# The pooling layer of a four-part decoder step: trailing sums on one engine, one channel group after the other

## The reference

```
h = rmsnorm(x, norm_mix)                        # x: rows x 2048
ext = concat(15 earlier rows (zeros or the stored ones), h)
for g, w in enumerate((2, 4, 8, 16)):           # four groups of 512 channels = 4 tiles
    mean = (sum of the last w rows of ext) / min(w, pos + 1)
    d[g] = mean - h                             # for the group's channels
    y[g] = d[g] @ w_pool[g]                     # 512 x 512
x = x + y * scale
new pool state = last 15 rows of ext
```

## Time and profile before

| | us |
|---|---|
| median of 3 runs | 2839.45 (2839.45 to 2842.92) |
| the profiled execution | 2834.88 |
| its span | 2833.1 |
| PE busy in it | 2645.6 (93%) |
| DVE busy | 1637.4 (58%) |
| ACT busy | 1298.8 (46%) |
| POOL busy | 511.2 (18%) |

### The profile page before, as it was taken

One profiled execution on the slowest core, in us unless ns is written; L12 is line 12 of the kernel. 1 busy time (PEld: TensorE's weight loads), 2 busy tenths in 40 slices (PEclk: granted clock), 3 DMA queues, 4 the chain that ended last, 5 costly groups with the idle time before them and its releaser, 6 DMA issues.

```text
span 2833.1 us, 68041 instructions
## 1 busy us (share of the span) xinstructions
PE 2645.6 (93%) x25416; PEld 2545.9 (90%) x25416; DVE 1637.4 (58%) x2721; ACT 1298.8 (46%) x1995; POOL 511.2 (18%) x822
## 2 busy tenths in 40 slices
PE   3899999999999699999788888889999999999997
PEld 2899999999999699999677777779999999999997
DVE  7666546664565686533554554434766456654664
ACT  1566434443344355433454545533666344443542
POOL 4222102220022300000021222222222012200222
PEclk7999999999999899999899999979999999999998
DMA  3554444444444544454010001034545454555444
GB/s 114 171 165 156 162 157 156 155 159 159 150 162 136 179 139 152 156 160 150 8 33 30 26 26 37 22 140 141 179 159 171 163 164 161 164 165 166 159 146 142
DMA packets 113711, 378.13 MB, mean 133 GB/s; under 512 B 12080, under 2 KB 22960, under 8 KB 113328
## 3 DMA queue, kind: packets, MB, share of 16 engines
q1 hardware_dynamic: 113584, 376.26, 40.6%
HBM read 363.61 MB, written 12.60 MB: 133 GB/s over the span
## 4 chain that ended last, share of the span: by engine, by line
PE 87%; DVE 6%; ACT 2%; issue 2%; DMA 1%; POOL 1%; SPq 0%; DVEq 0%; ACTq 0%; POOLq 0%
PE bank L552 25%; PE bank L554 25%; PE bank L553 25%; PE bank L661 10%; DMA l<-L_all 1%; DVE pext L1391 1%; PE bank L632 1%; DVE ar L1324 1%; POOL sout L1620 0%; DVE h_lo L1194 0%; PE bank L787 0%; PE bank L796 0%; POOL vx L1581 0%; DVE gram L1339 0%; PE bank L616 0%
## 5 line engine op out<-in xcount | busy, mean ns | idle before, releaser
L1144 DVE TENSOR_TENSOR wlo<-raw,whi 128x1024 fp32r<-128x1024 f32 (+1 forms) x672 | 800.4, 1195 | 667.9 <-ACT whi L871 647.2
L552 PE MATMUL bank<-h_hi,whi 128*128 128x290 f32 (+1 forms) x3520 | 1060.5, 301 | 41.3 <-DVE h_lo L1170 26.3
L871 ACT ACTIVATE whi<-raw 128x1024 fp32r<-128x1024 f32 (+1 forms) x672 | 689.9, 1033 | 827.6 <-PE bank L554 818.4
L554 PE MATMUL bank<-h_hi,wlo 128*128 128x290 f32 (+1 forms) x3520 | 1057.5, 300 | 0.0
L553 PE MATMUL bank<-h_lo,whi 128*128 128x290 f32 (+1 forms) x3520 | 1056.7, 300 | 0.0
L552 PEld LDWEIGHTS bank<-h_hi,whi 128*128 128x128 f32 x3520 | 668.6, 190 | 44.8 <-issue 31.0
L553 PEld LDWEIGHTS bank<-h_lo,whi 128*128 128x128 f32 x3520 | 669.3, 190 | 0.1
L554 PEld LDWEIGHTS bank<-h_hi,wlo 128*128 128x128 f32 x3520 | 669.2, 190 | 0.0
L552 PE MATMUL bank<-act_hi,whi 128*128 128x304 f32 (+1 forms) x1376 | 410.1, 298 | 0.9 <-DVE act_lo L1253 0.9
L554 PE MATMUL bank<-act_hi,wlo 128*128 128x304 f32 (+1 forms) x1376 | 410.4, 298 | 0.0
L553 PE MATMUL bank<-act_lo,whi 128*128 128x304 f32 (+1 forms) x1376 | 409.7, 298 | 0.0
(11 more groups left out here) (210 smaller groups left out, 3055.9 us busy)
## 6 DMA issues: line engine op xcount, KB each, us to landing
raw<-W_all SPq DMA_DIRECT2D x648, 512.0 KB, 3.4
raw<-W_all SPq DMA_DIRECT2D x32, 192.0 KB, 3.2
wkv_out<-sout SPq DMA_DIRECT2D x16, 288.0 KB, 2.2
l<-L_all SPq DMA_DIRECT2D x16, 256.0 KB, 2.8
s<-wkv_st SPq DMA_DIRECT2D x16, 256.0 KB, 3.0
x<-xT SPq DMA_DIRECT2D x4, 608.0 KB, 6.0
x_spill<-x SPq DMA_DIRECT2D x1, 2432.0 KB, 7.2
x<-x_spill SPq DMA_DIRECT2D x1, 2432.0 KB, 9.8
```

The source lines that it names most:

```text
L552: mm_(acc, wh, xh, start=first, stop=False)
L554: return mm_(acc, wl, xh, start=False, stop=last)
L871: activation(WHI[q][:, 0:n], RAW[q][:, 0:n], ACT.Copy).then_inc(whi_ready, 1)
L1144: tt(WLO[q][:, 0:n], RAW[q][:, 0:n], WHI[q][:, 0:n].bitcast(f32), ALU.subtract).then_inc(wlo_ready, 1)
```

## The change

DVE makes all trailing sums; POOL's part is gone, and of the five buffers `win` two are left. ACT multiplies x by `mix0` into `pext` ahead of the norm, three tiles before the root and the rest after it. DVE then goes through the groups in the order 0 to 3: it multiplies four tiles at once by `rnorm`, makes the group's trailing sums and its differences, and goes on to the next. The mean and the subtraction are one operation with a constant, except for the first w - 1 prompt rows, whose counts differ. The pooled tiles of groups 0 and 1 are added to x in groups 2 and 3, ahead of the differences there. In the start of the MLP, two of the weight splits stand behind the last four tiles, on DVE and ACT alike.

```diff
-            for grp in (3, 2, 0, 1):
-                for k in range(4 * grp, 4 * grp + 4):
-                    stt(pext[:, k, POOL_STATE:POOL_STATE + PROMPT], prompt(x[:, k, :]), par("mix0", k), prompt(rnorm), ALU.mult, ALU.mult)
-                    ins = stt(ext_samples(pext[:, k, :], POOL_STATE)[:, :, POOL_STATE:], samples(x[:, k, :]),
-                              par("mix0", k), samples(rnorm), ALU.mult, ALU.mult)
-                ins.then_inc(pooled_norm, 1)
-            vec.wait_ge(pooled_norm, 4)
             for grp in range(4):
-                if grp < 2:
-                    src = windows(tt, grp, win, link)
-                else:
-                    vec.wait_ge(win_ready, 4 - grp)
-                    src = win[4] if grp == 3 else win[3]
...
+                vec.wait_ge(pre_scaled, 4 * grp + 4)
+                tt(hh[:, :, POOL_STATE:POOL_STATE + PROMPT], hh[:, :, POOL_STATE:POOL_STATE + PROMPT], over_tiles(prompt(rnorm)), ALU.mult)
+                rn = samples(rnorm).rearrange("p (o b) e -> p o b e", o=1).broadcast_to([128, 4, NSEQ, TSAMPLE])
+                link(tt(of_samples(hh), of_samples(hh), rn, ALU.mult))
+                src = windows(tt, grp, win, link)
+                if grp > 1:
+
+                    pooled_x(0, 2 * grp - 4)
+                    pooled_x(0, 2 * grp - 3)
+                pdiff = pdiff_all[:, rows4, :]
+                n = w - 1
+                tt(pdiff[:, :, 0:n], src[:, :, POOL_STATE:POOL_STATE + n], over_tiles(rcnt[:, grp, 0:n]), ALU.mult)
+                stt(pdiff[:, :, n:PROMPT], src[:, :, POOL_STATE + n:POOL_STATE + PROMPT], 1.0 / w,
+                    hh[:, :, POOL_STATE + n:POOL_STATE + PROMPT], ALU.mult, ALU.subtract)
                 for k in range(4):
...
+                    ins = stt(samples(pdiff[:, k, :]), ext_samples(src[:, k, :], POOL_STATE)[:, :, POOL_STATE:], 1.0 / w,
+                              ext_samples(hh[:, k, :], POOL_STATE)[:, :, POOL_STATE:], ALU.mult, ALU.subtract)
                 link(ins)
...
+                tt(pdiff[:, :, 0:n], pdiff[:, :, 0:n], hh[:, :, POOL_STATE:POOL_STATE + n], ALU.subtract).then_inc(pdiff_ready, 1)
             for q in range(4):
                 pooled_x(1, q)
                 residual_rests(0, 4 * q, 4 * q + 4)
+                if q < 2:
+                    split(G["in00"], "in00", q)
+            for q in (2, 3):
                 split(G["in00"], "in00", q)
```

On POOL the loop goes, and on ACT the products with `mix0` come in:

```diff
-            for grp in (3, 2):
-                pool.wait_ge(pooled_norm, 4 - grp)
-                windows(nc.gpsimd.tensor_tensor, grp, (win[2], win[4]) if grp == 3 else (win[3], win[2]), pool_link)
-                pool.sem_inc(win_ready, 1)
...
+            for k in range(3):
+                scaled_prompt(k)
             norm_root(0)
+            scaled_prompt(3)
+            act.wait_ge(pst_loaded, 32)
+            for k in range(4):
+                scaled_samples(k)
+            for k in range(4, KT):
+                scaled_prompt(k)
+                scaled_samples(k)
```

More of the change, by code:

```diff
@@ L210, in build @@
     pext = sb("pext", [128, KT, PEXT], at=at)
-    win = [sb(f"win{i}", [128, 4, PEXT], at=at) for i in range(5)]
+    win = [sb(f"win{i}", [128, 4, PEXT], at=at) for i in range(2)]
     rcnt = sb("rcnt", [128, 4, TOK], at=at)
@@ L298, in build @@
     x_loaded = [sem(f"x_loaded{i}") for i in range(4)]
-    squared, sq_used, pooled_norm, win_ready = [sem(n) for n in ("squared", "sq_used", "pooled_norm", "win_ready")]
+    squared, sq_used, pre_scaled = [sem(n) for n in ("squared", "sq_used", "pre_scaled")]
     prefix_set = [sem(f"prefix_set{i}") for i in range(2)]
@@ L1065, in _, with scaled_prompt, scaled_samples @@
             act.wait_ge(in_loaded, 32)
-            norm_root(0)
+            def scaled_prompt(k):
+                activation(pext[:, k, POOL_STATE:POOL_STATE + PROMPT], prompt(x[:, k, :]), ACT.Copy, scale=par("mix0", k))
+            def scaled_samples(k):
+                activation(ext_samples(pext[:, k, :], POOL_STATE)[:, :, POOL_STATE:], samples(x[:, k, :]), ACT.Copy,
+                           scale=par("mix0", k)).then_inc(pre_scaled, 1)
+            for k in range(3):
+                scaled_prompt(k)
+            norm_root(0)
+            scaled_prompt(3)
[5 more added lines that the diff above has]
+                scaled_samples(k)
             act.sem_inc(whi_ready, end("pool"))
@@ L1394, in _, with over_tiles @@
-            vec.wait_ge(pooled_norm, 4)
-            for grp in range(4):
-                if grp < 2:
-                    src = windows(tt, grp, win, link)
-                else:
-                    vec.wait_ge(win_ready, 4 - grp)
-                    src = win[4] if grp == 3 else win[3]
[L1401 to L1404, removed]
+            def over_tiles(a):
+                return a.rearrange("p (o t) -> p o t", o=1).broadcast_to([128, 4, a.shape[-1]])
@@ L1405, in _ @@
                 for k in range(4):
-                    ins = ts(samples(pdiff[:, k, :]), ext_samples(src[:, k, :], POOL_STATE)[:, :, POOL_STATE:],
-                             1.0 / WINDOWS[grp], None, ALU.mult)
+                    ins = stt(samples(pdiff[:, k, :]), ext_samples(src[:, k, :], POOL_STATE)[:, :, POOL_STATE:], 1.0 / w,
+                              ext_samples(hh[:, k, :], POOL_STATE)[:, :, POOL_STATE:], ALU.mult, ALU.subtract)
                 link(ins)
-                tt(pdiff[:, :, 0:PROMPT], pdiff[:, :, 0:PROMPT], hh[:, :, POOL_STATE:POOL_STATE + PROMPT], ALU.subtract)
@@ L1410, in _ @@
-                for k in range(4):
-                    ins = tt(samples(pdiff[:, k, :]), samples(pdiff[:, k, :]),
-                             ext_samples(hh[:, k, :], POOL_STATE)[:, :, POOL_STATE:], ALU.subtract)
-                ins.then_inc(pdiff_ready, 1)
-                if grp in (1, 2):
-                    pooled_x(0, 2 * grp - 2)
-                    pooled_x(0, 2 * grp - 1)
+                tt(pdiff[:, :, 0:n], pdiff[:, :, 0:n], hh[:, :, POOL_STATE:POOL_STATE + n], ALU.subtract).then_inc(pdiff_ready, 1)
```

5 lines of the change are left out of this document (added).

## The result

The changed kernel took 2817.53 us (median of 4 runs, 2815.72 to 2819.18), the one before, run beside it, 2841.18 (2839.45 to 2843.79): a ratio of 0.9921, 95% interval 0.9909 to 0.9934, or some 22 us less. The profiled execution took 2815.72 with a span of 2813.9; before it was 2834.88 and 2833.1.

The account below looks back on a forecast made before the run. DVE's norm, blocked by POOL's sums, kept PE waiting. Last difference 17.0 us earlier, MLP start 18.1, less 0.3 for weights: 17.8 gained, so 2817.1 against the profiled execution, 2821.7 as median, range 2814 to 2829.

Parts of the forecast that it names:

- Up to the first multiply: nothing moves: Start of the norm: DVE's first multiply still starts at 20.18, with 0 to 2 us late as the range.
- ACT's products in time: ACT's multiplies of x by the norm weights: ready before DVE's groups want them, the last by 31 us at most.
- The groups: DVE's norm, sums and differences by channel group: 5.63, 7.64, 12.37 and 14.38 us, in all 40.0 if POOL rests.
- POOL's squares: POOL's additions of pooled tiles' squares beside DVE in groups 2 and 3: cost 1.6 us a group, bounds 0 and 3.3.
- The 2.5 a group: Skill page's whole-instruction exclusion applied to three POOL additions in groups 2 and 3: 2.5 us each group, end 1.8 later.
- The last difference: End of DVE's differences, ahead of the last pooling products: ready at 63.4 against 80.37, 17.0 us earlier.
- TensorE: Pooling products: start near 26, gaps of some 3 and 8 us ahead of the last two groups, end near 74.
- The rival that has the clock low through all of group 3: Last pooling group after its gap: 16.4 us in place of 10.6, gain 12, total 2827.5; chance 0.07.
- the one in which it stays low through all four groups: All 128 pooling products at half clock: 65 us, ending at 91, no change at 2839; chance 0.06.
- it lasts on into the MLP: Low clock in the MLP's first group: 96 products take 24.3 us in place of 16.5, slower at 2847; chance 0.03.
- The tail: From the last difference to PE's first MLP product: 17.2 us where it took 18.31, so the MLP starts at 80.6.
- The string of store and weights: Pool store, then loads for the second MLP group: weights at 97.0 to 97.6, wanted at 97.1; 0.3 us lost.

Follow-up runs that it names:

- dve_norm: Changed kernel with DVE's two norm multiplies a tile in place of ACT's products; ratio 0.9951 to the kernel before.
- no_early_squares: Changed kernel with POOL leaving the squares of tiles 0 to 7 out of the next norm's sum (output not the reference's); ratio 0.9915 to the kernel before.
- splits_back: Changed kernel with the weight splits of the MLP's first group back in each round of four tiles; ratio 0.9927 to the kernel before.
- loads_ahead: Changed kernel with the second MLP group's first two weight loads ahead of the pool store in SyncE's queue; ratio 0.9921 to the kernel before.
- sums_to_dve: Kernel before, with POOL's trailing sums made by DVE and nothing else changed; ratio 0.9971 to the kernel before.
- fed_sized: Changed kernel with 8 idle TensorE products ahead of group 3 and 16 ahead of the MLP; median 2822.3 us, ratio 0.9934 to the kernel before.
- fed_gap: Changed kernel with 16 idle TensorE products ahead of pooling group 3; ratio 0.9935 to the kernel before.
- fed_mlp_diff: Changed kernel with groups 2 and 3's pooled tiles behind their differences and 16 idle TensorE products ahead of the MLP; 2817.37 us, ratio 0.9926.

## Why the prediction was right, step by step

The forecast was 2821.7 in 2814 to 2829, faster at 0.91. It was made against the profiled execution as 2817.1, and that took 2815.72: 1.4 us less.

- **Up to the first multiply: nothing moves.** Wrong by 0.85 us, in the change's favour. ACT's timeline:

```profile
14.58 1.33 ACT L1069 ACTIVATE pext<-x,par 128x272 f32<-128x272 f32 x3
15.92 1.28 ACT L876 ACT_TABLE_LOAD   x1
17.21 0.46 ACT L876 ACTIVATE rnorm<-meansq 128x304 f32<-128x304 f32 x1
```

  Before, ACT idled 2.08 us until `meansq` was there and then loaded the table. Now the load follows the three products at once, at 15.92, ahead of `meansq`, which starts at 16.21 on DVE. From there to the first multiply it takes 3.58 us; before, with `meansq` at 15.75, it took 4.43. In dve_norm, without the products, it takes 4.42. Why the load does not wait when products stand ahead of it the trace does not say.
- **ACT's products in time.** Right: the small ones take 0.21 each end to end (four in 0.94), and all are done by 26.5, against 31 at most.
- **The groups.** 5.43 and 7.44 against 5.63 and 7.64. Without POOL's squares groups 2 and 3 take 12.20 and 14.17 (no_early_squares), against 12.37 and 14.38. The new operation takes 1.20 to the next start (reckoned 1.27), the four small ones 0.53 with their wait (0.69).
- **POOL's squares.** Reckoned 1.6 a group in bounds of 0 and 3.3; measured 1.38 and 1.26. Group 2's share is read off the longer operations: 0.42 for 0.19, 1.12 for 0.49, 0.70 for 0.19, in all 1.37. Three additions do fall in, each costs DVE only what is left of it when DVE asks, and the third addition is held up itself by the long DVE operation between 43.31 and 44.56:

```profile
42.51 0.83 POOL L1573 TENSOR_TENSOR sumsq<-sumsq,mix 128x304 f32<-128x304 f32 x1 [0.18 <-POOL sumsq L1573]
43.52 1.73 POOL L1573 TENSOR_TENSOR sumsq<-sumsq,mix 128x304 f32<-128x304 f32 x1 [0.18 <-ACT mix L1052]
```

  By the Trainium skill, page "SBUF — State Buffer", section "Who interferes with whom", the one that comes second waits until the other's instruction is over. By that rule, the trace agrees: 1.73 for 0.83 on one side, 0.49 to 1.12 on the other. The 2.5 a group that the prediction set beside it took each addition as wholly in DVE's way, and that did not happen.
- **The last difference** came at 61.78 and not 63.4: 0.4 from the start (0.85 less 0.46 of a later norm in this run), about 0.8 from four groups at 0.2, about 0.5 from POOL.
- **TensorE.** Gaps of 1.95 and 5.33 where I had 3 and 8: the clock was low in group 2 as well (0.68 in the mean from 46 to 50), which took 10.11 and not 8.2, and that is most of what the second gap is shorter by. Group 3 took 11.41 for 10.3 to 10.9: the clock was low for some 6 us, and I had taken 4.3 to 5.5. The rival that has the clock low through all of group 3 fell: it rose at 68 in the rows above. So did the one in which it stays low through all four groups, at 0.51 a product (the 64 of groups 0 and 1 took 19.04 us and not 33), and the one in which it lasts on into the MLP (there it rose at 85).
- **The tail** to the MLP, 17.2 reckoned, took 78.94 - 61.78 = 17.16.
- **The string of store and weights.** The mechanism was right, and it is what ends last now: splits_back and loads_ahead show it. The loss was sized too small, 0 to 0.5 against a stall of 0.83. The split was done at 96.05 (94.82 + 1.23), where I had 97.0 to 97.6. But I had measured the 1.1 us to spare to the end of the split, and TensorE waits for the bank that DVE empties behind it. DVE's timeline, first before, then after:

```profile
114.07 0.43 DVE L1207 TENSOR_TENSOR uext<-bank,rnorm 128x272 f32<-128x272 f32 x1
114.42 0.18 DVE L1208 TENSOR_TENSOR uext<-bank,rnorm 128x32 f32<-128x32 f32 x1
```

```profile
94.82 1.23 DVE L1166 TENSOR_TENSOR wlo<-raw,whi 128x1024 fp32r<-128x1024 f32 x1 [2.61 <-ACT whi L871]
95.96 0.43 DVE L1229 TENSOR_TENSOR uext<-bank,rnorm 128x272 f32<-128x272 f32 x1
96.31 0.18 DVE L1230 TENSOR_TENSOR uext<-bank,rnorm 128x32 f32<-128x32 f32 x1
```

  Before, the bank was empty at 114.60, so some 0.6 us were to spare and not 1.1.

Up to the second MLP group the change gave 115.22 - 96.61 = 18.6 us for 17.8 reckoned. Behind that nothing new came: the landmark is 18.5 earlier.

The measured time fell by more than these steps give. The medians differ by 23.65 us, the two profiled executions by 19.16, the landmarks by 18.48. The ratio's interval, some 19 to 26 us, still holds the 19.16. So the steps account for some 19 us. The other 4 to 5 are the distance of the median from the profiled execution, 6.3 before and 1.8 after; no row here shows a cause for that, and the spread of the executions is as large.

Where the prediction was furthest off is a step that has nothing to do with the kernel's work: I put the median 4.6 us above the profiled execution, as before; it stood 1.8 above. The range held because it left 4.6 us for a low run; that is room for the spread, and no merit of the steps.

The parts at the landmark, with the start of each run's norm taken off (16.47, 16.95, 17.04 and 16.21 against 15.75): POOL's sums on DVE alone 8.1 us, the order alone 2.1, the change with DVE's own norm 14.3, the whole change 18.9. So ACT's products are worth 4.6, which are the 3.8 on DVE and the 0.85 of the table load. That the order gives more once POOL rests is not shown: 14.3 - 8.1 = 6.2 is left for it, the single multiply-and-subtract and the moved splits. The moved splits gave nothing at the landmark (splits_back). The single operation and its small ones take DVE 1.89 us a group (23.33 to 25.22) where product and subtraction took 3.30 (52.24 to 55.54): 5.6 in four groups. And DVE's wait of 2.78 us for TensorE's products, ahead of the second pair of pooled tiles in sums_to_dve, is gone in the changed kernel. No run changes one of these two alone, so how the 6.2 divide stays open.

## What to carry to other kernels

An engine that helps can cost more than it does: look for short operations on the busy engine that take as long as one of the helper's, and reckon what giving the work back would save. When the stage is shortened, follow the transfers that hang on its end, for here the store and the loads behind it, late by no more than 1 us, kept what a moved split would have won. Where executions differ by more than the effect, measure at a landmark in the trace, and take the start's own difference off.

## What the runs showed of the hardware

- Behind a rest of 1.95 us between groups TensorE was at the lower level for a part of group 2 (mean granted clock 0.68 from 46 to 50): the group took 10.11 us for its 32 products. Behind 0.30 us in no_early_squares and 1.76 us in fed_sized the clock stayed at 1.00, and the group took 8.43 and 8.42. Where idle products left no rest ahead of the real ones, these ran at the full clock (group 3 in 8.35 us in fed_gap and fed_sized, the 54 MLP products in 6.90 and 6.81 in fed_sized and fed_mlp_diff). Where the idle ones ran over, the real ones started later by as much (3.55 us in fed_gap).
- In fed_sized and fed_mlp_diff feeding moved the landmark and not the median, and so did the other order of loads in loads_ahead. Landmark to the first MLP product behind the RWKV layer took 1853.55 - 971.56 = 881.99 us in the changed kernel, 881.54 before, but 890.1, 889.1 and 889.0 in fed_sized, loads_ahead and fed_mlp_diff. From 1300 to 1850 us, a stretch of many small products, the mean granted clock was 0.94 in the changed kernel and 0.93, 0.93 and 0.92 in those three. The relation is not a clean one (no_early_squares had 0.94 and 885.1 us, fed_gap 0.94 and 880.7, the kernel before 0.96). And these are single profiles: in all three kernels the profiled execution is the longest of five (2823.49, 2821.76 and 2820.26 us, the shortest being 2815.85, 2812.72 and 2813.84), while the changed kernel was profiled in its shortest. So the longer stretch may be that of a long execution and not of the kernel; whether it depends on when the stretch begins was not tried.
